# Gate products of a recurrent block as three rounded products, with their matrices divided on GpSimd

## The chip, the cores and the metric

The kernel runs on one core of a Trainium2 chip. A core has five engines that run their own instruction streams and meet at semaphores: TensorE (PE; weight loads are shown apart, as PEld), VectorE (DVE), ScalarE (ACT), GpSimd (POOL) and SyncE (SP), which issues all the transfers. The metric is device time in microseconds (us), smaller is better.

## The reference

One layer of a hybrid backbone is computed for 1024 latent and 256 context tokens (1280 columns in all, width 1024): a modulated RMSNorm, a combined input projection, three token mixers (Hyena, FNet, a recurrent block), three gates, an output projection, a second norm and a SwiGLU FFN. What is changed belongs to the recurrent block:

```python
xr = depthwise_conv(u_rx, rcw, rcb, ...)             # 4 taps
# per direction (fwd, bwd), in 8 blocks of 128 channels:
r = sigmoid(einsum('blnc,ncd->blnd', xb, w_r) + b_r)
i = sigmoid(einsum('blnc,ncd->blnd', xb, w_i) + b_i)
log_a = -RG_C * r * softplus(-lam)
a, mult = exp(log_a), sqrt(-expm1(2.0 * log_a))
h = scan(a, mult * (i * x))
y_c = ((h_f + h_b) * gelu(u_ry)) @ w_c
```

## The kernel before

Activations lie with 128 channels on the partitions and the 1280 tokens along a row, in three pieces of 512, 512 and 256 (`PIECES`, L23), one PSUM bank each. The projection streams its weights in tiles of 128x1024. POOL divides each tile in two: `w_hi` is the tile rounded to the format `fp32r`, `w_lo` the remainder (`split`, L806, its two instructions on L809 and L812). TensorE multiplies with `split_product` (L849): three matmuls on rounded operands, hi*hi, hi*lo and lo*hi, in one accumulation. A tile of the projection is 72 such matmuls, 24 to a piece.

The stage around the change is the second (`l2`), about 424 to 785 us of the span. It has 8 chunks of 128 channels, in pairs, n = 0 to 7. For chunk n TensorE does (`l2_pair`, L1049): projection tile 16+2n, on odd n the token products of FNet (L1045), tile 17+2n, the 12 gate units of the chunk (L1063: two directions, two matrices, three pieces) and on even n the channel products of FNet (L1032). The gate units are plain `f32` matmuls of `rpack` (four 128x128 matrices, and behind them the taps, biases and first states as 11 columns) with `xr`; each of them shows as two matmul records in the trace. Units go through five PSUM banks in turn (`MixUnits`, L237).

ACT copies tile 16+2n into `rin` (`into_padded`, L1391), on odd n takes FNet's token products, applies gelu to tile 17+2n into `g_ry` (L1482), the sigmoids to the gate units (L1493), then exp, tanh and square (L1501 to L1504) and sqrt (L1507). DVE makes `xr` from `rin` (`conv_chunk`, L2006; the convolution's instructions are on L1899 and L1904) and runs the scans (`scan_part`, L2013, scans on L2022). In one chunk DVE's order is: scan of direction 0, convolution of the next chunk, scan of direction 1, sums; ahead of an odd chunk FNet's first stage (`fnet_first_stage`, L1996) stands before that. SP loads `rpack` of chunk n+1 when chunk n-1 is finished (L684), and `v_b` for the next stage behind the other constants of that stage (L679).

Everything is ordered by hand. An engine takes its instructions in the order written and waits on semaphores, so an instruction that waits holds all that stand behind it on its engine. The steps that follow speak of: TensorE's wait for `xr_ready` (L1058), POOL's wait for the end of the tile two before (L821), and ACT's waits ahead of the gelus.

Of the kernel before, what the change touches and what calls it, by code (L numbers as in the profile page):

```python
# [57 lines left out]
R_CONV, R_CONVB, R_BR, R_BI, R_ST = 512, 516, 517, 519, 521  # L58
R_ALL = 523
# [234 lines left out]
def build_program(nc, dr):  # L294

    ctx = ExitStack()
    with ctx:
# [81 lines left out]
        rpack = [sb(st, f"rpack{s}", [P, R_ALL]) for s in range(2)]  # L379
# [3 lines left out]
        g_ry.append(sb(st, "g_ry1", [P, T]))  # L383
        st.close()
# [6 lines left out]
        fn_c = sb(st, "fn_c", [P, NT, 2, P])  # L391
        st.close()
# [82 lines left out]
        fin_stored, y_stored = sem("fin_stored"), sem("y_stored")  # L475
# [35 lines left out]
        xr_ready, xr_used = sem("xr_ready"), sem("xr_used")  # L511
        a2_ready = sem("a2_ready")
# [13 lines left out]
        sq1_ready, sq_summed = sem("sq1_ready"), sem("sq_summed")  # L526
# [8 lines left out]
        diag3_ready, rstd3_ready, ident_again = sem("diag3_ready"), sem("rstd3_ready"), sem("ident_again")  # L535
# [57 lines left out]
        def _(sp):  # L593
# [56 lines left out]
            load_taps(0)  # L650
            load_ahead(0, 0)
# [6 lines left out]
            sp.wait_ge(mod_ready, ROWS_FIRST + 8)  # L658
            sp.wait_ge(k_stored, 16 * 9)
            sp.dma_start(rpack[0][:], dr["rpack"][0]).then_inc(rpack_in[0], 16)  # L660
            sp.dma_start(fn_ch[:], dr["fn_ch"]).then_inc(fn_const_in, 16)
            sp.dma_start(fn_t[:], dr["fn_t"]).then_inc(fn_const_in, 16)

            def l2_chunk(n):

                m, s = n // 2, n % 2
                load_ahead(2 * n + L2_TILE0, 0)
                load_ahead(2 * n + (L2_TILE0 + 1), 1)
                if s:
                    sp.wait_ge(mix_free[u2.bank(FN2_UNIT + 2)], u2.nth(m, FN2_UNIT + 2) + 1)  # L670
                    sp.dma_start(dr["zb_s"][m], fn_y).then_inc(zb_stored, 16)
                    sp.wait_ge(zb_stored, 16 * m + 32)
                    if n < KD - 1:
                        sp.dma_start(fn_u[:], dr["hy_s"][m + 13]).then_inc(fn_in, 16)
                    else:
                        sp.dma_start(ident3[:], dr["ident"]).then_inc(hy_const_in, 16)
                        sp.dma_start(fwd3[:], dr["fwd"]).then_inc(hy_const_in, 16)
                        sp.dma_start(inv[:], dr["inv"]).then_inc(hy_const_in, 16)
                        sp.dma_start(v_b[:], dr["hy_s"][0]).then_inc(v_in, 16)  # L679
# [38 lines left out]
            def l3_pass(c, first, last):  # L718
                t = 6 * c + L3_TILE0
                for order in range(2):  # L720
                    load_ahead(t + 3 * order, 3 * order % 2)
                    store_gate(c, 3 * order)
                    if first and order == 0:
                        sp.wait_ge(zc_ready, KD + 1)
                        sp.wait_ge(zc_stored, 16 * KD + 16)
                        sp.dma_start(dr["zc_s"][KD - 1], g_ry[1][:]).then_inc(zc_stored, 16)
                        sp.dma_start(dr["state_out"], fin[:]).then_inc(fin_stored, 16)
                        sp.wait_ge(zc_stored, 16 * (2 + KD))
# [50 lines left out]
            sp.dma_start(ident_end[:], dr["ident"]).then_inc(ident_again, 16)  # L779
# [10 lines left out]
            sp.wait_ge(fin_stored, 16)  # L790
            sp.wait_ge(y_stored, 16 * sum(len(parts) for parts in Y_PARTS))

        @block.gpsimd
        def _(pool):
# [10 lines left out]

            def split(t, slot, hi, lo):  # L806
# [11 lines left out]
            with pool.Fori(1, OUT_TILE0 // 2 + 1) as m:  # L818
                for s in range(2):

                    pool.wait_ge(proj_done[2], 2 * m + s)  # L821
                    split(2 * m + s, s, w_hi[s], w_lo[s])

# [22 lines left out]
        def _(pe):  # L846
# [445 lines left out]
        def _(act):  # L1292
# [153 lines left out]
            fn(sp_w[:, 4, :], sp_w[:, 3, :], ACT.Ln).then_inc(sp_act, 1)  # L1446

# [164 lines left out]
            for p, (a, e, _) in enumerate(PIECES):  # L1612
                for i in range(KD + 1):
                    if i < KD:
                        v = KD * p + i
                        act.wait_ge(o_free[v % OUT_BANKS], v // OUT_BANKS + 1)
                        if i >= 2:
# [3 lines left out]
                           ACT.Square).then_inc(sq1_ready, 1)  # L1621
# [61 lines left out]
            def end_diag(p):  # L1683
# [4 lines left out]
                else:  # L1688
                    act.wait_ge(ident_again, 16)
# [35 lines left out]
        def _(dve):  # L1725
# [37 lines left out]
            def softplus(part):  # L1763
# [17 lines left out]
                if part == 2:  # L1781
# [6 lines left out]
                    own(ts(sp_neg[:], w[4], -RG_C, None, ALU.mult))  # L1788

# [146 lines left out]
            def l1_pass(i, units, it, last):  # L1936
# [16 lines left out]
                own.restart()  # L1953

# [51 lines left out]
            def conv_chunk(n, s, loads):  # L2006

                proj_taken(2 * n + (L2_TILE0 + 1))
                dve.wait_ge(rpack_in[s], loads)
                depthwise(xr, rin, lambda k: rpack[s][:, R_CONV + k:R_CONV + k + 1],  # L2010
                          rpack[s][:, R_CONVB:R_CONVB + 1], 4, 2, xr_ready)

            def scan_part(n, s, d):  # L2013
# [4 lines left out]
                own(tt(i_b[d][:], r_b[d][:], i_b[d][:], ALU.mult))  # L2018
                for a, e, seq in SEQS:
# [34 lines left out]
            conv_chunk(0, 0, 16)  # L2054
# [119 lines left out]
            def add_square(p, i):  # L2174
                a, e, _ = PIECES[p]
                dve.wait_ge(sq1_ready, KD * p + i + 1)
# [277 lines left out]
```

## Time and profile before

| | us |
|---|---|
| three timed runs | 2544.83, 2548.91 (median), 2552.96 |
| profiled execution, its own time | 2545.34 |
| its span | 2543.6 |
| TensorE busy | 2466.6 (97%) |
| DVE / ACT / POOL busy | 1420.8 / 613.9 / 682.8 |

The span runs from the first to the last instruction; the execution's own time lies 1.7 us above it. Busy matmuls overlap one another, so a rate of TensorE is read from the distance between the starts of two matmuls, not from their durations. The stretch before the first instruction of a row in which the engine stood idle is given in brackets with what ended it. The granted TensorE clock has two levels, 2.4 GHz (1.00 in a window) and 1.2 GHz.

### The profile page before, as it was taken

To read this page: it belongs to the slowest core of one execution; us is meant where nothing else is said; L and a number is where in the kernel's file an instruction comes from. 1 tells how busy PE (TensorE), PEld (TensorE's weight loads), DVE (VectorE), ACT (ScalarE), POOL (GpSimd) and SP (SyncE) were. 2 spreads that over 40 slices of the span, in tenths; PEclk is the share of its full clock that TensorE was granted. 3 is DMA by queue.
4 is the path that set the end of the run, shared out by engine and by line. 5 is a ranking of instruction groups with operands and counts; after the bars stand their busy time and mean duration, and the time that the engine had idled before them with its cause. 6 is when DMAs were issued, how large, how long until landed. Compare 5 with 4: busy or idle time off the path is not lost. (4 is left out here: it accounts for less than half of the span.)

```text
span 2543.6 us, 34536 instructions
## 1 busy us (share of the span) xinstructions
PE 2466.6 (97%) x13482; PEld 2094.6 (82%) x13482; DVE 1420.8 (56%) x2694; ACT 613.9 (24%) x884; POOL 682.8 (27%) x300
## 2 busy tenths in 40 slices
PE   5999999999999999999899999999999999999997
PEld 3788888787878888888778878888888888888886
DVE  6887887687767666655753564633223332333226
ACT  5323233666563212212220012200000000000004
POOL 1222221222222222212134360343313422342320
PEclk9999999999999999999999999999999999999999
DMA  7344443211132232323372250111101110111002
GB/s 306 126 150 163 151 161 135 69 52 62 52 146 102 94 110 93 112 107 135 112 258 93 87 197 1 50 50 34 49 16 49 42 40 23 43 49 33 29 21 83
DMA packets 53835, 234.53 MB, mean 92 GB/s; under 512 B 6259, under 2 KB 8819, under 8 KB 48132
## 3 DMA queue, kind: packets, MB, share of 16 engines
q1 hardware_dynamic: 53764, 233.55, 25.5%
q8 instruction: 48, 0.79, 0.1%
q14 instruction: 23, 0.19, 0.0%
HBM read 179.00 MB, written 54.53 MB: 92 GB/s over the span
## 5 line engine op out<-in xcount | busy, mean ns | idle before, releaser
L851 PE MATMUL ps<-h_hi,w_hi 128*128 128x512 f32 (+1 forms) x2112 | 761.2, 360 | 15.8 <-DVE h_lo L1870 9.2
L852 PE MATMUL ps<-h_lo,w_hi 128*128 128x512 f32 (+1 forms) x2112 | 750.3, 355 | 0.0
L853 PE MATMUL ps<-h_hi,w_lo 128*128 128x512 f32 (+1 forms) x2112 | 750.2, 355 | 0.0
L809 POOL TENSOR_TENSOR w_hi<-w_raw,zero_col 128x1024 fp32r<-128x1024 f32 x96 | 203.1, 2116 | 1570.7 <-PE ps L853 1294.3
L851 PEld LDWEIGHTS ps<-h_hi,w_hi 128*128 128x128 f32 x2112 | 400.8, 190 | 81.3 <-issue 17.6
L853 PEld LDWEIGHTS ps<-h_hi,w_lo 128*128 128x128 f32 x2112 | 400.9, 190 | 56.9
L852 PEld LDWEIGHTS ps<-h_lo,w_hi 128*128 128x128 f32 x2112 | 401.1, 190 | 55.6 <-issue 0.2
L2231 DVE TENSOR_TENSOR a<-sil,ps 128x512 f32<-128x512 f32 (+1 forms) x66 | 39.5, 599 | 504.1 <-PE ps L853 501.8
L812 POOL TENSOR_TENSOR w_lo<-w_raw,w_hi 128x1024 fp32r<-128x1024 f32 x96 | 260.5, 2713 | 7.5
L2254 DVE SCALAR_TENSOR_TENSOR x<-ps,mod,x 128x512 f32<-128x512 f32 (+1 forms) x264 | 172.3, 661 | 98.1 <-PE ps L853 97.5
L852 PE MATMUL ps<-h_lo,wf_hi 128*128 128x512 f32 (+1 forms) x624 | 224.4, 360 | 0.0
L851 PE MATMUL ps<-h_hi,wf_hi 128*128 128x512 f32 (+1 forms) x624 | 223.1, 358 | 0.0
L853 PE MATMUL ps<-h_hi,wf_lo 128*128 128x512 f32 (+1 forms) x624 | 221.8, 355 | 0.0
L1642 ACT ACTIVATE sil<-ps 128x512 f32<-128x512 f32 (+1 forms) x66 | 34.6, 526 | 752.0 <-PE ps L853 751.8
L851 PE MATMUL ps<-act_hi,wf_hi 128*128 128x512 f32 (+1 forms) x528 | 187.2, 355 | 0.6 <-DVE act_lo L2237 0.6
L853 PE MATMUL ps<-act_hi,wf_lo 128*128 128x512 f32 (+1 forms) x528 | 187.0, 354 | 0.0
L852 PE MATMUL ps<-act_lo,wf_hi 128*128 128x512 f32 (+1 forms) x528 | 186.9, 354 | 0.0
L809 POOL TENSOR_TENSOR wf_hi<-w_raw,zero_col 128x1024 fp32r<-128x1024 f32 x48 | 94.6, 1972 | 181.2 <-PE ps L853 181.2
L851 PEld LDWEIGHTS ps<-h_hi,wf_hi 128*128 128x128 f32 x624 | 117.2, 188 | 20.4 <-issue 0.2
L852 PEld LDWEIGHTS ps<-h_lo,wf_hi 128*128 128x128 f32 x624 | 117.5, 188 | 18.3 <-issue 0.2
L853 PEld LDWEIGHTS ps<-h_hi,wf_lo 128*128 128x128 f32 x624 | 117.1, 188 | 18.6
L812 POOL TENSOR_TENSOR wf_lo<-w_raw,wf_hi 128x1024 fp32r<-128x1024 f32 x48 | 116.3, 2422 | 3.8
(279 smaller groups left out, 3441.5 us busy)
## 6 DMA issues: line engine op xcount, KB each, us to landing
w_raw<-in_weights SPq DMA_DIRECT2D x146, 512.0 KB, 3.8
ada_w<-in_w_ada SPq DMA_DIRECT2D x18, 1024.0 KB, 7.9
scratch_gate_s<-g_st SPq DMA_DIRECT2D x24, 640.0 KB, 3.3
side<-scratch_gate_s SPq DMA_DIRECT2D x24, 640.0 KB, 3.9
scratch_k_s<-kstage SPq DMA_DIRECT2D x8, 1536.0 KB, 6.7
hy_k<-scratch_k_s SPq DMA_DIRECT2D x8, 1536.0 KB, 8.8
scratch_hy_s<-hout SPq DMA_DIRECT2D x16, 640.0 KB, 3.1
ada_early<-in_w_ada SPq DMA_DIRECT2D x6, 1024.0 KB, 22.1
```

Of the source, the lines that this page charges most:

```text
L809: nc.gpsimd.tensor_tensor(hi[:], w_raw[slot % 2][:], zero_col[:].to_broadcast([P, D]), ALU.add).then_inc(pool_step, 1)
L812: nc.gpsimd.tensor_tensor(lo[:], w_raw[slot % 2][:], hi[:].bitcast(F32), ALU.subtract).then_inc(split_done, 1)
L851: mm(out, w_pair[0], x_pair[0], start=first, stop=False)
L852: mm(out, w_pair[0], x_pair[1], start=False, stop=False)
L853: return mm(out, w_pair[1], x_pair[0], start=False, stop=last)
L1642: fn(sil[n % 2][:, 0:e - a], ps[b][:, 0:e - a], ACT.Silu).then_inc(f_free[b], 1)
L2231: tt(a32[n % 2][:, 0:e - a], sil[n % 2][:, 0:e - a], ps[ub][:, 0:e - a], ALU.mult).then_inc(f_free[ub], 1)
L2254: stt(x1[:, m, a:e], ps[b][:, 0:e - a], mod[:, 5 * KD + m, seq:seq + 1], x1[:, m, a:e], ALU.mult, ALU.add).then_inc(f_free[b], 1)
```

## The change

The gate products become `split_product`s. ACT rounds `xr` to `xr_hi` (one instruction over 1280 columns, written behind `take_fnet_tokens` and ahead of the gelus), DVE subtracts to get `xr_lo` in two parts (`split_chunk`), POOL divides the four matrices of a chunk into `r_hi` and `r_lo` (`split_gates`, 512 columns each). The parameters of a chunk are now two transfers, 11 columns of `rpack` and 512 of `r_mats`; those of chunk 0 are loaded before the first stage's loop. The convolution of chunk 0 stands in the last pass of the first stage. FNet's first input `fn_u` is issued ahead of FNet's constants, which no longer wait for the stored filters; `v_b` is issued after the last chunk's `xr` was used. Some semaphores are merged.

```diff
             def load_gates(n):
+                sp.dma_start(rpack[n % 2][:], dr["rpack"][n][:, R_MATS:R_MATS + R_VECS]).then_inc(rpack_in[n % 2], 16)
+                if n:
+                    sp.wait_ge(r_split, n)
+                sp.dma_start(r_mats[:], dr["rpack"][n][:, 0:R_MATS]).then_inc(rpack_in[n % 2], 16)
...
             load_taps(0)
+            load_gates(0)
             load_ahead(0, 0)
...
-            sp.wait_ge(mod_ready, ROWS_FIRST + 8)
-            sp.wait_ge(k_stored, 16 * 9)
-            sp.dma_start(rpack[0][:], dr["rpack"][0]).then_inc(rpack_in[0], 16)
-            sp.dma_start(fn_ch[:], dr["fn_ch"]).then_inc(fn_const_in, 16)
-            sp.dma_start(fn_t[:], dr["fn_t"]).then_inc(fn_const_in, 16)
...
-                    sp.dma_start(rpack[1 - s][:], dr["rpack"][n + 1]).then_inc(rpack_in[1 - s], 16)
+                    load_gates(n + 1)
...
             sp.dma_start(fn_u[:], dr["hy_s"][12]).then_inc(fn_in, 16)
+            sp.dma_start(fn_ch[:], dr["fn_ch"]).then_inc(fn_const_in, 16)
+            sp.dma_start(fn_t[:], dr["fn_t"]).then_inc(fn_const_in, 16)
+            sp.wait_ge(k_stored, 16 * 9)
             for n in range(KD):
                 l2_chunk(n)
+            sp.wait_ge(xr_used, KD)
+            sp.dma_start(v_b[:], dr["hy_s"][0]).then_inc(v_in, 16)
...
+            def split_gates(n):
+                pool.wait_ge(rpack_in[n % 2], 32 * (n // 2) + 32)
+                if n == 0:
+                    pool.wait_ge(proj_done[2], L2_TILE0 + 2)
+                else:
+                    j = RG_UNIT[(n - 1) % 2] + 11
+                    pool.wait_ge(mix_done[u2.bank(j)], u2.nth((n - 1) // 2, j) + 1)
+                r_done.append(n)
+                nc.gpsimd.tensor_tensor(r_hi[:], r_mats[:], zero_col[:].to_broadcast([P, R_MATS]),
+                                        ALU.add).then_inc(pool_step, 1)
+                pool.wait_ge(pool_step, L2_TILE0 + 2 * n + 2 + len(r_done))
+                nc.gpsimd.tensor_tensor(r_lo[:], r_mats[:], r_hi[:].bitcast(F32), ALU.subtract).then_inc(r_split, 1)
+            for n in range(KD):
+                tile_pair(L2_TILE0 // 2 + n)
+                split_gates(n)
...
                     projection_tile(2 * n + (L2_TILE0 + 1), 1)
-                    pe.wait_ge(xr_ready, n + 2)
-                    pe.wait_ge(rpack_in[s], 16 * m + 16)
+                    pe.wait_ge(r_split, n + 1)
+                    pe.wait_ge(xr_split, n + 1)
                     for j in range(12):
                         out, done = mix_unit(u2, m, RG_UNIT[s] + j)
                         a, e, _ = PIECES[j % 3]
-                        mm(out[:, 0:e - a], rpack[s][:, (j // 3) * P:(j // 3 + 1) * P], xr[:, a:e],
-                           start=True, stop=True).then_inc(done, 1)
+                        at = slice((j // 3) * P, (j // 3 + 1) * P)
+                        split_product(out[:, 0:e - a], [r_hi[:, at], r_lo[:, at]],
+                                      [xr_hi[:, a:e], xr_lo[0][:, a:e] if a < LAT else xr_lo[1][:, a - LAT:e - LAT]],
+                                      True, True).then_inc(done, 1)
...
                         take_fnet_tokens(m)
+                    act.wait_ge(xr_ready, n + 2)
+                    fn(xr_hi[:], xr[:], ACT.Copy).then_inc(xr_rounded, 1)
                     act.wait_ge(zc_stored, 16 * n + 16)
...
                 else:
                     zero_edges()
+                    conv_chunk(0, 0, 32)
                 ada_add(units, it, 8, 2 * i + ADA_FIRST, 4)
...
+            def split_chunk(n):
+                dve.wait_ge(xr_rounded, n + 1)
+                own.add(tt(xr_lo[0][:], xr[:, 0:LAT], xr_hi[:, 0:LAT].bitcast(F32), ALU.subtract))
+                own.add(tt(xr_lo[1][:], xr[:, LAT:T], xr_hi[:, LAT:T].bitcast(F32), ALU.subtract))
+                own.settle()
+                dve.sem_inc(xr_split, 1)
...
                     scan_part(n, s, 0)
                     if not (last and s):
-                        conv_chunk(n + 1, 1 - s, 16 * m + 16 * (s + 1))
-                    scan_part(n, s, 1)
+                        conv_chunk(n + 1, 1 - s, 32 * m + 32 * (s + 1))
+                        scan_part(n, s, 1, lambda: split_chunk(n + 1))
+                    else:
+                        scan_part(n, s, 1)
...
-            conv_chunk(0, 0, 16)
+            dve.wait_ge(k_stored, 16 * 9)
+            split_chunk(0)
             fnet_first_stage(0)
```

In `scan_part` the new argument is called between the product that makes `i_b` and the two scans. Where instructions move, the streams of before and of the changed kernel read so. First DVE, from the last rows of a chunk's convolution of the next `xr` to the scans of direction 1; before:

```order
L1904 SCALAR_TENSOR_TENSOR xr<-rin,rpack,xr 128x1024
L1904 SCALAR_TENSOR_TENSOR xr<-rin,rpack,xr 128x256
L2017 MEMSET r_b 128x1
L2018 TENSOR_TENSOR i_b<-r_b,i_b 128x1280
L2022 SCALAR_TENSOR_TENSOR t_b<-a_b,rpack,i_b 128x1024
L2022 SCALAR_TENSOR_TENSOR t_b<-a_b,i_b 128x256
```

and in the changed kernel:

```order
L1948 SCALAR_TENSOR_TENSOR xr<-rin,rpack,xr 128x1024
L1948 SCALAR_TENSOR_TENSOR xr<-rin,rpack,xr 128x256
L2070 MEMSET r_b 128x1
L2071 TENSOR_TENSOR i_b<-r_b,i_b 128x1280
L2061 TENSOR_TENSOR xr_lo<-xr,xr_hi 128x1024
L2062 TENSOR_TENSOR xr_lo<-xr,xr_hi 128x256
L2077 SCALAR_TENSOR_TENSOR t_b<-a_b,rpack,i_b 128x1024
L2077 SCALAR_TENSOR_TENSOR t_b<-a_b,i_b 128x256
```

Two subtractions stand between the product and the scans; TensorE's gate units wait for them. Next POOL in the second stage, where it had only tile after tile; in the changed kernel one chunk reads:

```order
L825 TENSOR_TENSOR w_hi<-w_raw,zero_col 128x1024
L828 TENSOR_TENSOR w_lo<-w_raw,w_hi 128x1024
L825 TENSOR_TENSOR w_hi<-w_raw,zero_col 128x1024
L828 TENSOR_TENSOR w_lo<-w_raw,w_hi 128x1024
L849 TENSOR_TENSOR r_hi<-r_mats,zero_col 128x512
L852 TENSOR_TENSOR r_lo<-r_mats,r_hi 128x512
```

The two rows on `r_mats` are new and stand behind the split of tile 17+2n. Last SP at the end of the second stage, from the constants of the third (`ident`, `fwd`, `inv`) on; before:

```order
L676 DMA ident<-in_ident 128x128
L677 DMA fwd<-in_fwd 128x4608
L678 DMA inv<-in_inv 128x4608
L679 DMA v_b<-scratch_hy_s 128x1280
L687 DMA scratch_zc_s<-g_ry 128x1280
L596 DMA w_raw<-in_weights 128x1024
```

and in the changed kernel:

```order
L687 DMA ident<-in_ident 128x128
L688 DMA fwd<-in_fwd 128x4608
L689 DMA inv<-in_inv 128x4608
L697 DMA scratch_zc_s<-g_ry 128x1280
L708 DMA v_b<-scratch_hy_s 128x1280
L604 DMA w_raw<-in_weights 128x1024
```

`v_b` moved behind a store that waits for a finished chunk, and the next weight tile (tile 34) now stands behind `v_b` and its wait.

## Rows read from the trace of the kernel before

**Rows 1.** A stretch: busy us of each engine, granted clock, transfers' share, GB/s.

```profile
450.00:500.00 50.00, 48.63 (x238) 39.78 (x239) 35.67 (x45) 26.41 (x35) 9.24 (x4) 0.97 0.22 77
```

**Rows 2.** What TensorE waited for, 380 to 800 us: total, times, longest.

```profile
PE ps L1032 <- issue: 4.4, 1, 4.4
PE ps L1063 <- ACT r_b L1493: 1.1, 3, 0.4
```

**Rows 3.** TensorE in order of time: start us, length us, instructions merged.

```profile
438.15 8.86 PE L1063 MATMUL ps<-xr,rpack 128*128 128x512 f32 x24 [0.48 <-DVEq L1907]
451.37 8.83 PE L1032 MATMUL ps<-fn_ch,fn_a 128*128 128x256 f32 x32 [4.36 <-issue]
459.85 0.58 PE L851 MATMUL ps<-h_hi,w_hi 128*128 128x512 f32 x1
...
462.31 0.39 PE L852 MATMUL ps<-h_lo,w_hi 128*128 128x512 f32 x1
462.54 0.39 PE L853 MATMUL ps<-h_hi,w_lo 128*128 128x512 f32 x1
...
471.04 0.28 PE L852 MATMUL ps<-h_lo,w_hi 128*128 128x256 f32 x1
471.16 0.28 PE L853 MATMUL ps<-h_hi,w_lo 128*128 128x256 f32 x1
...
492.06 8.76 PE L1063 MATMUL ps<-xr,rpack 128*128 128x512 f32 x24
500.46 0.58 PE L851 MATMUL ps<-h_hi,w_hi 128*128 128x512 f32 x1
...
528.76 8.32 PE L1063 MATMUL ps<-xr,rpack 128*128 128x512 f32 x22
...
538.03 7.17 PE L1032 MATMUL ps<-fn_ch,fn_a 128*128 128x256 f32 x32
544.86 0.58 PE L851 MATMUL ps<-h_hi,w_hi 128*128 128x512 f32 x1
```

**Rows 4.** VectorE in order of time, chunk 1, and in it the convolution for chunk 2.

```profile
485.91 2.35 DVE L2022 TENSOR_TENSOR_SCAN t_b<-a_b,rpack,i_b 128x1024 f32<-128x1024 f32 x1
...
523.15 5.12 DVE L1904 SCALAR_TENSOR_TENSOR xr<-rin,rpack,xr 128x1024 f32<-128x1024 f32 x6
528.54 1.49 DVE L2018 TENSOR_TENSOR i_b<-r_b,i_b 128x1280 f32<-128x1280 f32 x1
530.07 3.86 DVE L2022 TENSOR_TENSOR_SCAN t_b<-a_b,rpack,i_b 128x1024 f32<-128x1024 f32 x1
533.86 2.77 DVE L2022 TENSOR_TENSOR_SCAN t_b<-a_b,i_b 128x256 f32<-128x256 f32 x1
```

**Rows 5.** GpSimd in order of time, the split of tile 23.

```profile
529.09 2.70 POOL L809 TENSOR_TENSOR w_hi<-w_raw,zero_col 128x1024 fp32r<-128x1024 f32 x1 [8.10 <-PE ps L853]
531.86 4.21 POOL L812 TENSOR_TENSOR w_lo<-w_raw,w_hi 128x1024 fp32r<-128x1024 f32 x1
```

**Rows 6.** ScalarE in order of time: first sigmoids of chunk 1, then its exp.

```profile
494.48 1.63 ACT L1493 ACTIVATE r_b<-ps,rpack 128x512 f32<-128x512 f32 x3
...
501.49 1.28 ACT L1501 ACT_TABLE_LOAD   x1
```

**Rows 7.** ScalarE by line: busy us, mean ns; a rounding of 1280 columns.

```profile
L1597 ACT ACTIVATE h_hi<-x 128x1280 fp32r<-128x1280 f32 x8 | 10.2, 1276 | 149.7 <-DVE x L2147 149.7
```

**Rows 8.** VectorE in order of time: FNet's first stage, chunk 0.

```profile
439.47 0.69 DVE L223 TENSOR_TENSOR fn_c<-fn_u 128x512 f32<-128x512 f32 x1 [1.43 <-DMA fn_u<-scratch_hy_s]
```

**Rows 9.** VectorE in order of time: the last use of `xr` is done here.

```profile
765.67 1.49 DVE L2038 SCALAR_TENSOR_TENSOR r_b<-r_b,t_b 128x1280 f32<-128x1280 f32 x1 [0.92 <-ACT r_b L1504]
```

**Rows 10.** TensorE in order of time: first work of the third stage.

```profile
769.54 1.25 PE L1092 MATMUL ps<-ident,v_b 128*128 128x128 f32 x10
...
800.82 3.52 PE L966 MATMUL ps<-hy_a,fwd 128*128 128x128 f32 x16 [2.74 <-ACT hy_z L1557]
```

**Rows 11.** Transfers: KB each, median us to landing.

```profile
side<-scratch_gate_s SPq DMA_DIRECT2D x24, 640.0 KB, 3.9
```

More of the change, by code:

```diff
@@ L56 @@
 V_ALL = V_SEL + 2
-R_CONV, R_CONVB, R_BR, R_BI, R_ST = 512, 516, 517, 519, 521
-R_ALL = 523
+R_MATS = 512
+R_CONV, R_CONVB, R_BR, R_BI, R_ST = 0, 4, 5, 7, 9
+R_VECS = 11
 TILES_L1, TILES_L2, TILES_L3 = 16, 16, 24
@@ L378, in build_program @@
         xr = sb(st, "xr", [P, T])
-        rpack = [sb(st, f"rpack{s}", [P, R_ALL]) for s in range(2)]
+        xr_lo = [sb(st, "xr_lo0", [P, LAT], F32R)]
+        sb(st, "under_r_b", [P, 32])
         for buf, name in ((r_b, "r_b"), (i_b, "i_b"), (a_b, "a_b")):
@@ L383, in build_program @@
         g_ry.append(sb(st, "g_ry1", [P, T]))
+        xr_hi = sb(st, "xr_hi", [P, T], F32R)
+        xr_lo.append(sb(st, "xr_lo1", [P, CTX], F32R))
+        r_mats = sb(st, "r_mats", [P, R_MATS])
+        rpack = [sb(st, f"rpack{s}", [P, R_VECS]) for s in range(2)]
         st.close()
@@ L391, in build_program @@
         fn_c = sb(st, "fn_c", [P, NT, 2, P])
+        r_hi, r_lo = sb(st, "r_hi", [P, R_MATS], F32R), sb(st, "r_lo", [P, R_MATS], F32R)
         st.close()
@@ L511, in build_program @@
         xr_ready, xr_used = sem("xr_ready"), sem("xr_used")
+        xr_rounded, xr_split, r_split = sem("xr_rounded"), sem("xr_split"), sem("r_split")
         a2_ready = sem("a2_ready")
@@ L678, in l2_chunk @@
                         sp.dma_start(inv[:], dr["inv"]).then_inc(hy_const_in, 16)
-                        sp.dma_start(v_b[:], dr["hy_s"][0]).then_inc(v_in, 16)
                 if n:
@@ L789, in _ @@
                     sp.dma_start(dr["y"][:, lo:hi, a:e], x1[:, lo:hi, a:e]).then_inc(y_stored, 16)
-            sp.wait_ge(fin_stored, 16)
-            sp.wait_ge(y_stored, 16 * sum(len(parts) for parts in Y_PARTS))
+            sp.wait_ge(y_stored, 16 + 16 * sum(len(parts) for parts in Y_PARTS))
         @block.gpsimd
@@ L804, in _ @@
             pool.wait_ge(consts_set, 3)
+            r_done = []
             def split(t, slot, hi, lo):
@@ L816, in _, with tile_pair @@
             split(1, 1, w_hi[1], w_lo[1])
-            with pool.Fori(1, OUT_TILE0 // 2 + 1) as m:
+            def tile_pair(m):
                 for s in range(2):
@@ L822, in _ @@
                     split(2 * m + s, s, w_hi[s], w_lo[s])
+            def split_gates(n):
[10 more added lines that the diff above has]
+                nc.gpsimd.tensor_tensor(r_lo[:], r_mats[:], r_hi[:].bitcast(F32), ALU.subtract).then_inc(r_split, 1)
+            with pool.Fori(1, L2_TILE0 // 2) as m:
+                tile_pair(m)
+            for n in range(KD):
+                tile_pair(L2_TILE0 // 2 + n)
+                split_gates(n)
+            with pool.Fori(L3_TILE0 // 2, OUT_TILE0 // 2 + 1) as m:
+                tile_pair(m)
             chunks = [2] * TILES_A + [1] * TILES_C + [2] * TILES_A
@@ L1446, in _ @@
             fn(sp_w[:, 4, :], sp_w[:, 3, :], ACT.Ln).then_inc(sp_act, 1)
+            act.wait_ge(sp_ready, 3)
             act.wait_ge(k_stored, 16 * 9)
@@ L1620, in _ @@
                         fn((sq_o if i else sq_sum)[:, a:e], x1[:, OUT_ORDER[p][i], a:e],
-                           ACT.Square).then_inc(sq1_ready, 1)
+                           ACT.Square).then_inc(sq_ready, 1)
                     if p:
@@ L1688, in end_diag @@
                 else:
-                    act.wait_ge(ident_again, 16)
+                    act.wait_ge(ident_in, 32)
                 for t in range((e - a) // P):
@@ L1788, in softplus @@
                     own(ts(sp_neg[:], w[4], -RG_C, None, ALU.mult))
+                    dve.sem_inc(sp_ready, 1)
             for k in range(1, KD):
@@ L1953, in l1_pass, with conv_chunk @@
                 own.restart()
+            def conv_chunk(n, s, loads):
+                proj_taken(2 * n + (L2_TILE0 + 1))
+                dve.wait_ge(rpack_in[s], loads)
+                depthwise(xr, rin, lambda k: rpack[s][:, R_CONV + k:R_CONV + k + 1],
+                          rpack[s][:, R_CONVB:R_CONVB + 1], 4, 2, xr_ready)
             def zero_edges():
@@ L2004, in fnet_first_stage, with scan_part @@
                 dve.sem_inc(fna_ready, 1)
[L2006 to L2013, printed above, removed]
+            def split_chunk(n):
[4 more added lines that the diff above has]
+                dve.sem_inc(xr_split, 1)
+            def scan_part(n, s, d, then=None):
                 dve.wait_ge(root_ready, 2 * n + (d + 1))
@@ L2018, in scan_part @@
                 own(tt(i_b[d][:], r_b[d][:], i_b[d][:], ALU.mult))
+                if then:
+                    then()
                 for a, e, seq in SEQS:
@@ L2175, in add_square @@
                 a, e, _ = PIECES[p]
-                dve.wait_ge(sq1_ready, KD * p + i + 1)
+                dve.wait_ge(sq_ready, KD * (p + 1) + i + 1)
                 if i >= 2:
```

13 lines of the change are left out of this document (7 added, 6 removed).

## The prediction

> **What bounds the kernel now.** I read the page first: TensorE is busy 97% of the span, no other engine over 56%. So time is gained by fewer or cheaper matmuls and lost by anything that lets TensorE wait. The second view is what TensorE waited for in the stage that the change touches: one wait of 4.4 us at FNet's channel products of chunk 0, and three of 0.4 us in gate units [rows 2]. Hence the stage runs at TensorE's pace, and the third view, TensorE in order of time, gives that pace [rows 3]. Let G be the start of chunk 1's gate units, 492.06. They last to 500.46, 8.40 us. Two tiles follow, to 528.76: G+36.7. Chunk 2's gate units last 9.27 (to 538.03); the 0.87 above 8.40 is TensorE held up by the sigmoids. FNet's channel products take 6.83 (538.03 to 544.86).
>
> The fourth view is DVE beside POOL, which shows how close the rest is. The convolution for chunk 2 ends at 523.15+5.12 = 528.27, G+36.2 [rows 4], and TensorE needs it at G+36.7. From an odd chunk to an even one the slack is half a microsecond. There are three such transitions (1 to 2, 3 to 4, 5 to 6); from an even chunk to an odd one FNet's products on TensorE give several microseconds more.
>
> **Cheaper gate units.** A rounded product starts 0.23 us after the one before at 512 columns and 0.12 us at 256 (462.31 to 462.54, 471.04 to 471.16) [rows 3]. A chunk has 8 wide and 4 narrow units of three products: 24 x 0.23 + 12 x 0.12 = 6.9 us for 8.40. So 1.5 us less per chunk, 12 us over eight chunks, if nothing waits. The sigmoids keep up: three of them take 1.63 us, of which some 0.1 overlaps the next three, where three units now take 1.7 [rows 6].
>
> **From an odd chunk to the next.** What TensorE needs is now later by three steps: rounding on ACT, which must follow the convolution, then two subtractions on DVE, which stand behind the product that makes `i_b`. First when the convolution ends. Sigmoids began at G+2.4 and the exp at G+9.4 [rows 6]; twelve of them need 4 x 1.5 = 6.0, so exp comes at about G+8.5, 0.9 earlier, and with it DVE's scans and the convolution. I give 0.2 back because POOL's split of tile 22 then meets the scans a little earlier: convolution over at G+35.5. Meanwhile tile 21 ends at 36.7-1.5 = G+35.2. Rounding 1280 columns costs 1.28 [rows 7]; it ends at G+36.9 and lies beside DVE's product (1.49, from 0.27 after the convolution [rows 4]), which ends at G+37.3. The trace has no such subtraction; the product of 1280 columns takes 1.49 [rows 4], so by the column I take 1.2 and 0.3, plus 0.2 to settle.
>
> Now POOL. It starts to split tile 23 0.33 after TensorE ends tile 21 (529.09 against 528.76) [rows 3, 5], in the changed kernel at G+35.5, just when DVE wants its product. Rows 4 and 5 show what comes of that. DVE's product is over at 530.03, POOL's first half at 531.79, the scan at 533.93, POOL's second half at 536.07, the short scan at 536.63: they take turns, 1.8, 2.1, 2.1 and 0.6 us apart. The long scan shows 3.86, against 2.35 alone [rows 4]. The two subtractions now stand where the two scans stood, so each waits for one half of POOL's split: 37.3+1.8+1.2+2.1+0.3+0.2 = G+42.9. TensorE was ready at G+35.2: it waits 7.7 us. If they did not take turns it would be G+39.0 and a wait of 3.8. I take 7.7, since these are the same kind of instruction in the same place as the rows.
>
> The Trainium skill (SBUF — State Buffer, section Who interferes with whom) says the same more generally: a DVE instruction with two SBUF inputs and a GpSimd one that reads SBUF exclude each other for their whole length, and the order of issue decides who is blocked. It speaks against this change, which puts two such subtractions on TensorE's path; with its rule the wait is that of the turns, with engines that merely share it is the shorter one. The trace agrees in rows 4 and 5.
>
> After a wait TensorE is also slow: behind 4.36 us of idleness the channel products took 8.48 (451.37 to 459.85) where the same work takes 6.83 [rows 3], and the granted clock of 450 to 500 us is 0.97 [rows 1], so part of it lay at 1.2 GHz instead of 2.4. I charge 1.5 us per wait (bounds 0 and 1.7).
>
> One transition then costs 7.7+1.5 and saves 1.5 (chunk 1's units), 1.5 (chunk 2's) and the 0.87 at the end of chunk 2's units, since the scan that those sigmoids waited for is done before they begin. Net +5.3, three times: +16. Behind it, even to odd: the convolution for chunk 3 follows its tile, and rounding and subtractions add about 3 us to a slack of more than that; I charge nothing. Were that cover gone, each of four would cost at most 3 us. Splitting the matrices on POOL (two of 512 columns, about 2 us a chunk) falls behind the gate units of the chunk before; nobody waits for it but DVE's FNet stage, which has 4 us of slack to ACT's exps. The new transfers are 11 and 512 columns where there were 523 and have a whole chunk to land: nothing.
>
> **The start.** Chunk 0's gate units waited 0.5 us for the convolution [rows 3], which now is done in the first stage: -0.6. The units save 1.5. Then TensorE waited 4.4 for FNet's first stage, which began only at 439.47, when `fn_u` had landed behind the constants [rows 8]. `fn_u` is now issued ahead of them and some 6 us earlier. DVE must do the convolution, softplus and subtractions first and reach FNet's stage at about 436. Alone it takes some 6 us; before it took until 451.2 because two splits of POOL fell into it. These fall into it again, one or two us later. The stage ends between 442 and 448, TensorE is ready at 437.5+6.9 = 444.4. I take 446.5 for the channel products' start: 4.9 us before 451.37. With a shorter wait the slow clock gives back half of its 1.65: -0.8. Sum of the start -5.7 (bounds -8.6 and -3.4).
>
> **The end of the stage.** Chunk 7's units save 1.5. The transposes that followed at 769.54 need `v_b` [rows 10], which so far was long there. It is now issued when DVE has passed its last use of `xr`, at 765.67+1.49 = 767.2 before [rows 9]; TensorE's clock at that place gains 1.5 and DVE's chain 0.9, so in the new frame DVE comes 0.6 later against TensorE. A transfer of its size lands in 3.9 us [rows 11]: 767.2+0.6+0.1+3.9 = 771.8, a wait of 2.2 for TensorE. Behind it stood another wait of 2.7 [rows 10] for the stores and ACT copies that follow DVE's last chunk; that chain hardly moves, so this wait shrinks by about what TensorE lost. -1.5+2.2-0.7 = 0 (bounds -1.5 and +4, the latter if 2.2 us of waiting also bring the low clock, or the weight tile queued behind `v_b` is late).
>
> **Sum.** -5.7+16+0 = about +10 us on the profiled execution's own 2545.3, which is 2556. That execution lies 3.6 below the median of the three runs, 2548.9, which a measurement of the changed kernel will be held against; so 2548.9+10.3 = 2559.
>
> **Rivals.**
> 1. No turns. The subtractions pass before POOL's halves, or POOL starts late: wait 3.8, still with the low clock. Per transition 3.8+1.5-3.9 = +1.4, in all +4.2-5.7 = -1.5: 2547. For it: the two are issued back to back and the margins are tenths. Against: the two scans in the same place let POOL in between.
> 2. The other side: the wait is hidden. If the conversions were through when tile 21 ends, each transition would save 3.9, the start 5.7 and the end 1.5: -19, 2530. It decides at a convolution that ends 3.5 us earlier than the one I worked out. Against: that end hangs on ACT's sigmoids and exps, which gain 0.9. A weaker form, wait 3.8 at full clock and the best start, gives -9: 2540.
> 3. Worse: even-to-odd transitions wait as well (up to 4 x 3), or the low clock also catches the end: +20, 2569.
> 4. The chain of the start gains nothing, as FNet's stage meets both splits in full: forecast +2, inside its range.
>
> **How the numbers follow.** What a measurement tells from no change is 0.3%, 7.6 us: bounds 2541.3 and 2556.5. Forecast 50% (own range 2553 to 2566, nine in ten of it slower), rival 1 25% (same, for the most part), rival 2 with its weaker form 13%, rival 3 12%. Slower: 0.45+0.12+0.02 = 0.59. Faster: 0.10+0.04 = 0.14. Same: 0.27. The range is 2540 to 2569, from the weaker form of rival 2 to rival 3.
>
> **What would show it.** Right: three waits of TensorE of about 8 us at the first gate product of chunks 2, 4 and 6, put down to the subtraction on DVE; there the subtraction of 1024 columns shows about 3 us instead of 1.2; gate units of 6.9 us on odd chunks; a wait of about 2 us for `v_b`; channel products of chunk 0 before 448. Wrong: waits near 4 us (rival 1), none (rival 2), gate units clearly over 7 us without waits (then a rounded product is not the price), or waits on chunks 3, 5, 7 (rival 3).

## The result, and the profile after

The changed kernel takes 2557.1 us (median of 16 runs, 2554.7 to 2562.0), the kernel before 2548.8 (16 runs, 2544.8 to 2554.2). The ratio is 1.0034 with a 95% interval from 1.0027 to 1.0041: slower by a third of a per cent, 8.3 us. All times and ratios here are of executions at the full granted clock (0.98 to 0.99); one run each of e2 (3214.8 us) and e3 (2753.8) fell well below it and is left out. The profiled execution of the changed kernel has a span of 2553.5 us (own time 2555.4), 9.9 above that of before.

First TensorE's waits in the stage of the change, 380 to 830 us, in the changed kernel: total, times, longest. They answer to [rows 2].

```profile
PE ps L889 <- DVEq L2064: 19.7, 3, 6.6
PE ps L1004 <- ACT hy_z L1600: 2.5, 1, 2.5
PE ps L889 <- ACT rin L1435: 1.9, 3, 0.7
PE ps L1150 <- DVEq L2161: 0.8, 1, 0.8
```

The wait of 4.4 us for FNet's first stage is gone. Three waits of 6.6 have come, released by line 2064, the count that DVE raises behind the two subtractions. A small one is new as well: three times 0.7 for ACT's copy into `rin`.

TensorE in order of time shows where they stand, to be held against [rows 3]; start, length, and in brackets the idle time before.

```profile
439.54 0.39 PE L889 MATMUL ps<-xr_hi,r_hi 128*128 128x512 f32 x1
...
446.72 7.07 PE L1070 MATMUL ps<-fn_ch,fn_a 128*128 128x256 f32 x32
...
453.44 0.58 PE L889 MATMUL ps<-h_hi,w_hi 128*128 128x512 f32 x1
...
485.68 0.39 PE L889 MATMUL ps<-xr_hi,r_hi 128*128 128x512 f32 x1
...
492.86 0.40 PE L889 MATMUL ps<-h_hi,w_hi 128*128 128x512 f32 x1
...
528.14 0.79 PE L889 MATMUL ps<-xr_hi,r_hi 128*128 128x512 f32 x1 [6.59 <-DVEq L2064]
536.64 7.07 PE L1070 MATMUL ps<-fn_ch,fn_a 128*128 128x256 f32 x32
543.36 0.58 PE L889 MATMUL ps<-h_hi,w_hi 128*128 128x512 f32 x1
...
777.40 1.28 PE L1132 MATMUL ps<-ident,v_b 128*128 128x128 f32 x10 [0.30 <-issue]
```

G, the start of chunk 1's gate units, is now 485.68. Chunk 0's units last 446.72 - 439.54 = 7.18 and chunk 1's 7.18. Channel products of chunk 0 follow without a gap. Chunk 2's units start at G+42.5 (it was G+36.7) and last 8.50 where the same work takes 7.0 elsewhere; the granted clock from 520 to 545 us is 0.86, where it was 1.00 before.

VectorE and GpSimd around that wait, in the changed kernel, answer to [rows 4, 5].

```profile
507.45 3.86 DVE L2077 TENSOR_TENSOR_SCAN t_b<-a_b,rpack,i_b 128x1024 f32<-128x1024 f32 x1
511.24 2.81 DVE L2077 TENSOR_TENSOR_SCAN t_b<-a_b,i_b 128x256 f32<-128x256 f32 x1
...
515.65 5.12 DVE L1948 SCALAR_TENSOR_TENSOR xr<-rin,rpack,xr 128x1024 f32<-128x1024 f32 x6
...
521.04 1.49 DVE L2071 TENSOR_TENSOR i_b<-r_b,i_b 128x1280 f32<-128x1280 f32 x1
522.65 2.71 DVE L2061 TENSOR_TENSOR xr_lo<-xr,xr_hi 128x1024 fp32r<-128x1024 f32 x1
525.29 2.56 DVE L2062 TENSOR_TENSOR xr_lo<-xr,xr_hi 128x256 fp32r<-128x256 f32 x1
527.99 2.35 DVE L2077 TENSOR_TENSOR_SCAN t_b<-a_b,rpack,i_b 128x1024 f32<-128x1024 f32 x1
```

```profile
506.89 2.28 POOL L825 TENSOR_TENSOR w_hi<-w_raw,zero_col 128x1024 fp32r<-128x1024 f32 x1 [11.04 <-PE ps L891]
509.25 4.25 POOL L828 TENSOR_TENSOR w_lo<-w_raw,w_hi 128x1024 fp32r<-128x1024 f32 x1
521.63 2.65 POOL L825 TENSOR_TENSOR w_hi<-w_raw,zero_col 128x1024 fp32r<-128x1024 f32 x1 [8.13 <-PE ps L891]
524.36 3.20 POOL L828 TENSOR_TENSOR w_lo<-w_raw,w_hi 128x1024 fp32r<-128x1024 f32 x1
```

The engines take turns: product, POOL's first half, long subtraction, POOL's second half, short subtraction. The short one, of 256 columns, shows 2.56 us, most of it waiting. What the scans paid before the change, where TensorE lost at most the 0.87 us at the end of chunk 2's units to it, the subtractions pay now on TensorE's path. The same rows stand at chunks 4 and 6 (2.71 and 2.56 both times). The rows show a second such place that the prediction did not speak of: tile 22's split stretches the scans ahead of the convolution, 3.86 and 2.81 where they take 2.35 and 0.67 alone (first and last row of [rows 4] and of the fence above).

Three things differ outside. In the first filter pass TensorE waits 1.2 us for DVE's taps stage (`f_a`), which it did not before. The first matmul starts at 9.21 instead of 8.28, when its weights land. And the last weight products before the output projection took 40.6 us (1287.81 to 1328.42) for 39.1 (1280.15 to 1319.23). Across eleven profiles of this study that stretch took either 39.1 (three of them) or 40.5 to 40.6 (eight). The first value stands also in two experiments on the changed kernel (e6, e7), the second also in one on the kernel before (e8), so the change does not decide it; in the changed kernel's profile products of 512 columns start 0.43 us apart from 1289.12 to 1292.10, where they otherwise start 0.23 apart.

### The profile page after: what moved, and what is told of

It reads as the page before. It is cut to its first block and busy times, and to the rows that moved or that the text cites. A ratio compares the mean times of both kernels' runs of the same rounds, so it can differ in the third digit from the quotient of the medians.

```text
span 2553.5 us, 34777 instructions
## 1 busy us (share of the span) xinstructions
PE 2459.5 (96%) x13578; PEld 2110.0 (83%) x13578; DVE 1438.4 (56%) x2710; ACT 623.2 (24%) x892; POOL 706.0 (28%) x316
```

## The experiments

Four questions are behind them: are the turns with POOL the cause, or the length of the chain; what did the start give by itself, and through what; what do the loads that were moved cost; and does a version win that keeps the cheap products and avoids the turns.

**POOL holds back the second tile (e1).** In the program of POOL:

```
def tile_pair(m, held=None):
    for s in range(2):
        pool.wait_ge(proj_done[2], 2 * m + s)
+       if held and s == 1:
+           pool.wait_ge(xr_split, held)
        split(2 * m + s, s, w_hi[s], w_lo[s])
...
+   tile_pair(L2_TILE0 // 2 + n, n if n % 2 and n > 1 else None)
```

> The changed kernel, in which POOL splits the second tile of a pair (tile 23 and its like) only when DVE has subtracted xr for the next even chunk; transitions 1 to 2, 3 to 4 and 5 to 6. Theory (turns): POOL's split stands between DVE's two subtractions, so without it they show 1.2 and 0.4 us instead of 2.7 and 2.6, and TensorE's wait falls from 6.8 to about 3.2 us, three times: 11 us less than the changed kernel's 2557, about 2546, the low clock behind the wait as before. Rival (length of the chain): rounding, product and subtractions cost what they cost and POOL is only beside them: the wait stays at 6 to 7 us and the time at 2557 or 2556.

Measured: 2543.9 us, ratio to before 0.9988 (0.9979 to 0.9997). The subtractions, in order of time:

```profile
524.63 1.49 DVE L2073 TENSOR_TENSOR i_b<-r_b,i_b 128x1280 f32<-128x1280 f32 x1
526.24 1.23 DVE L2063 TENSOR_TENSOR xr_lo<-xr,xr_hi 128x1024 fp32r<-128x1024 f32 x1
527.38 0.42 DVE L2064 TENSOR_TENSOR xr_lo<-xr,xr_hi 128x256 fp32r<-128x256 f32 x1
527.95 4.08 DVE L2079 TENSOR_TENSOR_SCAN t_b<-a_b,rpack,i_b 128x1024 f32<-128x1024 f32 x1
```

and TensorE's wait for them:

```profile
PE ps L891 <- DVEq L2066: 8.9, 3, 3.1
```

1.23 and 0.42, and the wait falls from 6.6 to 3.1 (expected 3.2). No instruction of the chain changed; only POOL's moment did: its split of tile 23 begins at G+38.7 (G is 489.26 here) instead of G+35.9. The scan behind the subtractions now pays (4.08), where it costs TensorE 0.5 to 0.6 us of waiting for sigmoids. The time is 13 us below the changed kernel's. In the profiles the three waits give 10.8 of it (19.7 to 8.9), and the gate units of chunks 2, 4 and 6, where the low clock lies, 2.8 (27.0 to 24.2), those new waits included.

**POOL holds back both tiles (e2).** As above with `s == 0`, so that the split of tile 22 waits too.

> The changed kernel, in which POOL splits both tiles of the pair (22 and 23 and their like) only when DVE has subtracted xr for the next even chunk. Theory (turns): the scans ahead of the convolution show 2.35 and 0.67 us instead of 3.86 and 2.81, the convolution ends 3.6 us earlier (about G+31.6), the subtractions at about G+35.3, where tile 21 ends at G+35.6: no wait of TensorE and no low clock at chunks 2, 4 and 6, 3 x 8.3 = 25 us less than the changed kernel: about 2532. Rival: the convolution is released by something else (rin's copy on ACT, which has moved behind the square roots), so that it comes at most 1 us earlier: the time is that of the first experiment, about 2544 to 2546. A second rival: the held splits come so late that tile 22 or the gate matrices wait for them: over 2550.

Measured: 2533.8 us, ratio 0.9939 (0.9926 to 0.9952). VectorE:

```profile
511.41 2.35 DVE L2079 TENSOR_TENSOR_SCAN t_b<-a_b,rpack,i_b 128x1024 f32<-128x1024 f32 x1
513.68 0.67 DVE L2079 TENSOR_TENSOR_SCAN t_b<-a_b,i_b 128x256 f32<-128x256 f32 x1
...
515.95 5.12 DVE L1950 SCALAR_TENSOR_TENSOR xr<-rin,rpack,xr 128x1024 f32<-128x1024 f32 x6
```

G is 489.63 here; the convolution ends at 521.07, G+31.4 (expected G+31.6), instead of G+35.1. No wait for the subtractions is left on TensorE. The three waits and what came with them were 23 us.

**Without the subtractions (e6).** The product with `xr_lo` takes `xr_hi` once more, and DVE's two subtractions are left out.

```
-   own.add(tt(xr_lo[0][:], xr[:, 0:LAT], xr_hi[:, 0:LAT].bitcast(F32), ALU.subtract))
-   own.add(tt(xr_lo[1][:], xr[:, LAT:T], xr_hi[:, LAT:T].bitcast(F32), ALU.subtract))
-   own.settle()
...
-   [xr_hi[:, a:e], xr_lo[0][:, a:e] if a < LAT else xr_lo[1][:, a - LAT:e - LAT]],
+   [xr_hi[:, a:e], xr_hi[:, a:e]],
```

> The changed kernel without the subtractions on DVE that make xr_lo; TensorE does the same number of rounded products, the one with xr_lo taking xr_hi again, so this leaves the low part of xr out of the gate sums. Theory: TensorE then waits only for the rounding on ACT, which ended 0.9 us after tile 21: waits of about 1 us at chunks 2, 4 and 6 instead of 6.8, 3 x 5.9 = 18 us less, and a few us of low clock: 2536 to 2539. Rival (the three products themselves or the rounding are what costs): no more than 5 us less, 2552 or more.

Measured: 2536.8 us, ratio 0.9955 (0.9942 to 0.9968). TensorE's wait at that place:

```profile
PE ps L889 <- DVEq L2061: 4.0, 3, 1.3
```

1.3 where 1 was expected. What ended last in front of the count is not the rounding but DVE's product, which stands there too:

```profile
525.45 1.27 ACT L1521 ACTIVATE xr_hi<-xr 128x1280 fp32r<-128x1280 f32 x1 [12.68 <-DVEq L1951]
525.63 1.49 DVE L2068 TENSOR_TENSOR i_b<-r_b,i_b 128x1280 f32<-128x1280 f32 x1
```

Rounding is over at 526.72, the product at 527.12. So rounding and product together are the small part of the wait, and the three rounded products are not what makes the changed kernel slower: this kernel, too, does all of them and is faster than before.

**The subtractions ahead of the product (e9).**

```
-   scan_part(n, s, 1, lambda: split_chunk(n + 1))
+   split_chunk(n + 1)
+   scan_part(n, s, 1)
```

> The changed kernel with the two subtractions directly behind the convolution, ahead of the product that makes i_b, POOL's splits as they were. Theory (turns): DVE then waits some 1.3 us for the rounding, POOL has begun the first half of its split by then (521.63 in the changed kernel's profile), so the subtractions still end behind POOL's first and second half; taking away the 1.5 us product in front of them gives less than 0.5 us per transition: waits of 6.3 to 6.9, time 2555 to 2558. Rival (length of the chain): the product's 1.5 us leave TensorE's path: waits of 5.3 us, 4 to 5 us less, 2552 to 2553.

Measured: 2555.0 us, ratio 1.0030 (1.0018 to 1.0041); 2 us less than the changed kernel, as much as the three waits gave, but within what the times leave open (1.0027 to 1.0041 there). VectorE, POOL and TensorE's wait:

```profile
525.74 2.47 DVE L2061 TENSOR_TENSOR xr_lo<-xr,xr_hi 128x1024 fp32r<-128x1024 f32 x1 [1.40 <-ACT xr_hi L1521]
528.13 2.56 DVE L2062 TENSOR_TENSOR xr_lo<-xr,xr_hi 128x256 fp32r<-128x256 f32 x1
```

```profile
525.24 1.89 POOL L825 TENSOR_TENSOR w_hi<-w_raw,zero_col 128x1024 fp32r<-128x1024 f32 x1 [8.16 <-PE ps L891]
```

```profile
PE ps L889 <- DVEq L2064: 17.5, 3, 5.8
```

5.8 lies between my two numbers (6.3 and 5.3) and fits neither well. The product in front was 1.5 us long, and its removal gave 0.75 (the wait's 6.57 to 5.83). DVE stood idle for 1.40 until the rounding was done, so the long subtraction was ready only 0.5 us earlier (G+36.5 for G+37.0, G here being 489.24). POOL's first half had begun before it in either order of DVE (525.24 against 525.74, 521.63 against 522.65). What gave the 0.75 is that half: no product of DVE holds it up, it shows 1.89 for 2.65 and is over at G+37.9 for G+38.6, and the subtractions follow it. So the chain in front of the subtractions got shorter by more than the wait did; what counts is when POOL's half is through.

**The start alone (e3, and a look at it, e10).** The changed kernel with the f32 gate product of before; the subtractions and `split_gates` are left out as well:

```
-   fn(xr_hi[:], xr[:], ACT.Copy).then_inc(xr_rounded, 1)
-   pe.wait_ge(r_split, n + 1)
-   pe.wait_ge(xr_split, n + 1)
+   pe.wait_ge(xr_ready, n + 2)
+   pe.wait_ge(rpack_in[s], 32 * m + 32)
...
-   split_product(out[:, 0:e - a], [r_hi[:, at], r_lo[:, at]], ...)
+   mm(out[:, 0:e - a], r_mats[:, at], xr[:, a:e], start=True, stop=True).then_inc(done, 1)
```

> The changed kernel with the gate products of the kernel before: one f32 product per unit from xr and r_mats, no rounding, no subtractions, no division of the matrices; what moved ahead (parameters, first convolution, fn_u ahead of the constants) and v_b's load stay as in the changed kernel. It is the start by itself. Theory: the waits at chunks 2, 4 and 6 vanish and the gain of the start stays: the wait of 4.4 us at the channel products of chunk 0 falls below 0.5, its slow clock (1.6) and the wait for the first convolution (0.5) go, against 1 us for the gate loads ahead of tile 2 and about 0.5 for v_b: 5 us less than before, about 2543 to 2544. Rival: the start gained in the changed kernel because its gate units are cheaper, or v_b takes the gain back: 2547 or more.

Measured: 2543.3 us, ratio 0.9979 (0.9968 to 0.9990): 5.5 us gained by the start alone.

> Another look at the kernel of the third experiment (the start by itself), for its profile at the full clock. Theory: no wait over 0.3 us at the channel products of chunk 0, which take 6.8 us; gate units of chunk 0 take 8.4; v_b makes TensorE wait under 1 us after chunk 7; gate units of chunks 2, 4 and 6 wait for nothing but the sigmoids; 2540 to 2545. Rival: a wait of 1 us or more at chunk 0's channel products, so that the start gains less than 5 us.

Measured: 2544.1 us, one run. Of chunk 0, gate units start at 442.54 and channel products at 451.13 with no wait. The transposes with `v_b` waited 0.3 at most. The theory holds; what keeps this kernel from more is a wait of 3.7 us at `f_a` in the first stage (below), and one of 2.2 us at the third stage's inverse products, which is 0.5 to 0.8 in most other profiles.

**fn_u behind the constants again (e4).**

```
+   sp.wait_ge(k_stored, 16 * 9)
    sp.dma_start(fn_ch[:], dr["fn_ch"]).then_inc(fn_const_in, 16)
    sp.dma_start(fn_t[:], dr["fn_t"]).then_inc(fn_const_in, 16)
+   sp.dma_start(fn_u[:], dr["hy_s"][12]).then_inc(fn_in, 16)
```

(and the two lines removed from ahead of and behind them)

> The changed kernel with fn_u issued behind the FNet constants again, in the order of the kernel before. Theory: FNet's first stage on DVE begins at about 440 of the span instead of 436 and then meets POOL's split of a tile, so that TensorE waits 3 to 5 us for it at the channel products of chunk 0 and runs at the low clock behind it: 5 to 6 us more than the changed kernel, 2562 to 2563. Rival: the start's gain comes from the convolution that was moved ahead; then the order of the loads changes 2 us at most, 2557 to 2559.

Measured: 2565.7 us, ratio 1.0064 (1.0052 to 1.0077); 8.6 us more than the changed kernel, expected 5 to 6. VectorE, FNet's first stage in it, and then in the changed kernel:

```profile
442.78 0.69 DVE L224 TENSOR_TENSOR fn_c<-fn_u 128x512 f32<-128x512 f32 x1 [2.96 <-DMA fn_u<-scratch_hy_s]
...
446.44 2.49 DVE L227 TENSOR_TENSOR fn_c<-fn_c 128x128 f32<-128x128 f32 x1
448.85 1.98 DVE L224 TENSOR_TENSOR fn_c<-fn_c 128x128 f32<-128x128 f32 x1
```

```profile
435.78 0.69 DVE L224 TENSOR_TENSOR fn_c<-fn_u 128x512 f32<-128x512 f32 x1
...
437.73 0.28 DVE L227 TENSOR_TENSOR fn_c<-fn_c 128x128 f32<-128x128 f32 x1
437.93 0.28 DVE L224 TENSOR_TENSOR fn_c<-fn_c 128x128 f32<-128x128 f32 x1
```

Three additions of 128 columns, 0.28 us alone, show 2 to 2.5 among POOL's splits. TensorE at the channel products:

```profile
456.65 10.06 PE L1070 MATMUL ps<-fn_ch,fn_a 128*128 128x256 f32 x32 [5.58 <-issue]
...
466.36 0.58 PE L889 MATMUL ps<-h_hi,w_hi 128*128 128x512 f32 x1
```

5.6 of waiting, and then 9.7 for work that takes 6.7 in the changed kernel. From tile 17's first product to tile 18's it is 36.5 us (429.85 to 466.36), against 36.2 before and 27.8 in the changed kernel: all of the start's gain hangs on this load, and the low clock makes the wait half as dear again. `fn_u` is issued 6.1 us after tile 17's first product here (436.00), 6.7 before (430.30 against 423.63) and 0.6 in the changed kernel (426.26 against 425.66). The edit moves the load behind two things, the constants and SP's wait for the stored filters; this run does not tell them apart, but in the changed kernel the two constants are issued within 2.7 us of `fn_u` (426.26 to 428.97), so the wait is the larger part.

**The first gate loads behind weight tile 2 (e5), and with both tiles held (e7).**

```
    load_taps(0)
-   load_gates(0)
    load_ahead(0, 0)
+   load_gates(0)
```

> The changed kernel, in which SP issues the loads of the first gate parameters and matrices behind the load of weight tile 2 (load_ahead(0, 0)), not ahead of it. Theory: those two issues put the tile's load, POOL's split of it and with it DVE's first taps stage about 1 us back at 79 to 99 us of the span, which is the wait of 1.2 us at f_a on TensorE; it goes, and everything behind lies 1.1 us earlier: 2556 for 2557, to be read in the profile, since 1 us is below what the times tell. Rival: the 1.2 us come from how two executions differ at the start (first matmul at 9.2 instead of 8.3 us): the wait at f_a stays.

Measured: 2555.9 us, ratio 1.0035 (1.0022 to 1.0048); against the changed kernel no difference that the times tell, as foretold. SP, POOL and VectorE of the changed kernel at that place, then POOL and VectorE of this one:

```profile
78.61 0.43 SPq L637 DMA_DIRECT2D rpack<-in_rpack  x1
79.08 0.43 SPq L640 DMA_DIRECT2D r_mats<-in_rpack  x1
79.56 0.43 SPq L604 DMA_DIRECT2D w_raw<-in_weights  x1
...
85.25 1.89 POOL L825 TENSOR_TENSOR w_hi<-w_raw,zero_col 128x1024 fp32r<-128x1024 f32 x1 [32.92 <-DMA w_raw<-in_weights]
...
88.15 2.82 DVE L2027 TENSOR_TENSOR tsum<-taps 128x1280 f32<-128x1280 f32 x1
```

```profile
83.38 1.89 POOL L825 TENSOR_TENSOR w_hi<-w_raw,zero_col 128x1024 fp32r<-128x1024 f32 x1 [31.48 <-DMA w_raw<-in_weights]
...
87.38 1.70 DVE L2027 TENSOR_TENSOR tsum<-taps 128x1280 f32<-128x1280 f32 x1
```

Two issues ahead of the weight tile, 0.47 us each, put it back by 0.95; POOL's split moves with it into DVE's `tsum`, which grows by 1.1, and DVE's stage then runs into POOL's next split as well. The wait at `f_a` is there in every kernel with the loads ahead (1.2 in the changed kernel, 3.7 to 4.1 in e1, e2, e4, e6, e9 and e10) and in none with the loads behind (before, e5, e7, e8). Why it is 1.2 in one profile and about 4 in six: in the changed kernel three additions of 128 columns, begun at 99.09, 99.29 and 99.49, passed at 0.28 each while POOL's first half, begun at 98.95, stood 0.8 us (2.71 for 1.89), and only the stage's last instructions met it (2.05 for 0.35); in e1 the two halves came between the additions, which show 1.99 and 2.42. In e5's profile the clock took the gain back: the weight products ahead of that place lasted 15.9 us (84.85 to 100.79) for 14.0 in the changed kernel, at a granted clock of 0.85 for 1.00 (84 to 101 us).

> The second experiment (both splits held back) together with the first gate loads behind weight tile 2. Theory: the two are independent, the wait of 4 us at f_a in the first stage goes, where the low clock takes back part of it: 1 to 4 us less than 2533.8, 2530 to 2533, and so 0.6 to 0.7% below the kernel before. Rival: the low clock takes back all: 2534.

Measured: 2530.3 us, ratio 0.9929 (0.9917 to 0.9941), 3.5 below e2, though the runs of the two overlap (2527.7 to 2532.7 and 2531.3 to 2535.7): 18.5 us faster than the kernel before, 26.8 faster than the changed one. TensorE's waits of 380 to 830 us in it:

```profile
PE ps L1006 <- ACT hy_z L1602: 3.1, 1, 3.1
PE ps L891 <- ACT rin L1437: 2.0, 3, 0.8
PE ps L1152 <- DVEq L2163: 0.6, 1, 0.6
PE ps L891 <- ACT g_st L1578: 0.5, 1, 0.5
PE ps L891 <- ACT r_b L1538: 0.5, 3, 0.2
```

Nothing of DVE or POOL is left between the chunks.

**A control: the kernel before, with both tiles held (e8).** The same edit in the kernel before, held until the convolution is done (`xr_ready`).

> The kernel before, in which POOL splits tiles 22 and 23 and their like only when the convolution for the next even chunk is done. A control: is it the holding back that makes the second experiment fast, or its meeting with the longer chain of the changed kernel? Theory: before the change the convolution was in time for TensorE, so an earlier one (by 3.6 us) gives nothing but the 0.9 us at the end of the gate units of chunks 2, 4 and 6: 2546 to 2548, ratio 0.999 to 1.000. Rival: holding back is a gain of its own: 2544 or less.

Measured: 2545.1 us, ratio 0.9987 (0.9978 to 0.9995), between the two expectations. Chunk 2's gate units take 8.59 (529.41 to 538.00) for 9.27, and a pair of chunks 84.25 for 85.03: 0.8 us three times, 2.4 of the 3.7. The other 1.3 is within the interval. Holding back alone gives a tenth of a per cent; most of what e2 gained is the removal of a wait that only the changed kernel has.

## Why the prediction was right, point by point

Forecast 2559, measured 2557.1; the step that carried it, the turns with POOL, is confirmed by e1 and e2. Other terms erred in both directions, and that the sum comes so close is in part luck.

- **Cheaper gate units**, 6.9 for 8.40: measured 7.2 for chunks 0 and 1 and 7.0 for chunk 3. Right to 0.3. The prediction's own terms, 24 x 0.23 + 12 x 0.12, add to 6.96, not 6.9; the rest is 0.2 us that TensorE stands at the seventh unit of chunks 0 and 1 and not of chunk 3.
- **Odd chunk to even**, +5.3 each, +16: periods from one odd chunk's units to the next were 85.03 before and are 89.91, 90.76 and 89.82: +4.9, +5.7, +4.8, in all +15.4. The wait was 6.6 instead of 7.7. Its parts in order: convolution over at G+35.1 (35.5 predicted), product at G+36.8 (37.3), subtractions at G+42.2 (42.7). TensorE was ready at G+35.9 (35.2): 0.3 from units of 7.2 for 6.9, and 0.4 from a step that was missing, ACT's copy into `rin`, for which TensorE waits 0.7 where it waited 0.3. The turns, e1 and e2 show, are the cause: 3.5 us of each wait through the subtractions, and the other 3.1 through the scans ahead of the convolution, which had stood in the profile of before and which I took as given. The +15.4 is nearer to +16 than its terms are: I took the wait 1.1 too long, the low clock behind it on average 0.5 too short, and left the copy out.
- **The rule of turns.** By the Trainium skill (SBUF — State Buffer, section Who interferes with whom) the two engines exclude each other for a whole instruction, and the order of issue decides who is blocked. The traces agree: POOL's first half shows 2.65 us where DVE's product had begun 0.6 before it (521.04, 521.63), and 1.89 in e9, where no product was in its way.
- **Low clock behind a wait**, 1.5: measured 8.50 - 7.0 = 1.5 for chunk 2, 9.69 - 7.0 = 2.7 for chunk 4 (617.69 to 627.38), 8.77 - 7.0 = 1.8 for chunk 6. One sum for all was a little low.
- **The start**, -5.7: from tile 17's products (423.63 before, 425.66 after) to tile 18 (459.85, 453.44), 36.2 became 27.8: -8.4, at the edge of my bound. The failed step is "these fall into it again": FNet's stage was over at 439.8, when POOL's first split had run for 1 us, also because the stage takes 4.1 us alone (435.78 to 439.83) and not some 6. In e4 the stage does fall among the splits, and the gain is gone.
- **The end**, 0: chunk 7's units gave 1.4; the wait for `v_b` was 0.3 instead of 2.2. The step that failed is the moment of its issue. I took the end of DVE's last instruction on `r_b`, 1.5 us long; the count that SP waits for asks only that the product with `xr` ahead of it is done. In the changed kernel `v_b` is issued at 773.41, as that last instruction begins (773.35), and the transposes start 4.0 later. With 0.4 less from there to the third stage's forward products (30.9 us for 31.3) that is -1.6 in all.
- **Loads nobody waits for**, 0: wrong. "A whole chunk to land" held for seven of the eight loads; the first was moved past weight tile 2 in SP's queue, and this costs 1.3 in the profile, where six others show waits of about 4. In the times it is 1.2 (e5, too little to tell from nothing) to 3.5 (e7 against e2, whose runs overlap).

Sum of the profile: -8.4 + 15.4 - 1.6 + 1.3 = +6.7, and of the 0.9 at the first matmul 0.8 is left when the filter pass begins, so that the third stage's forward products come 7.5 later (808.27 for 800.82). The last 2.4 of the 9.9 lie behind; 1.5 of them are the weight products of 40.6 for 39.1. So the start and the end came out 4.3 better than forecast and the transitions 0.6, and what was not forecast cost 4.5: these cancel. Rival 1 (no turns) would have been e1's kernel, and it was forecast at 2547 and took 2544. Rival 2 (the wait hidden, 2530) is e2's and e7's: 2534 and 2530.

## What to carry to other kernels

When a conversion is put on the path of the engine that bounds, look at what the other engine on the same memory does in that very microsecond: in e1, 13 us of the loss came from a GpSimd split that could run 3 us later. A split that is made a whole tile ahead of its use has no reason to run as soon as its buffer is free; a wait for the right count made nobody wait for the splits here (e2, e7) and gave more than the change itself had lost. And a load that "has time" must still be followed past every issue behind it in its queue.

## What the runs showed of the hardware

- Where GpSimd and VectorE both have instructions with SBUF inputs at hand, they mostly take turns, and the one of VectorE that meets a GpSimd instruction waits for most of its length, however short it is itself: a subtraction of 256 columns showed 2.56 us for 0.42, three additions of 128 columns in e4 1.98 to 2.49 for 0.28. Not each of a train does: an addition between them kept its 0.28 (450.75 in e4), and in the changed kernel's filter pass three passed one after the other while a GpSimd instruction stood 0.8 us. A sum by the column hides what short instructions lose so.
- What TensorE loses behind a wait is not in proportion to it: 1.5, 2.7 and 1.8 us behind three waits of the same 6.6, 3.0 behind one of 5.6, and at `f_a` 1.5 (e1) and 2.9 (e2) behind 3.9 and 4.0, against 4.5 us for the same products without one. The granted clock of these stretches was 0.86 (520 to 545), 0.80 (605 to 630) and 0.83 (700 to 720): part of each at 1.2 GHz, the rest at 2.4.
- Three rounded products with `xr` and the matrices cost 7.0 to 7.2 us a chunk where one f32 product costs 8.4.
